# A two-block model kernel: the first half of x loaded in two pieces

## What is computed

```python
x = jax.random.normal(ks[0], (BATCH, SEQ, D_MODEL), f32)      # 1 x 256 x 1024
for layer in range(DEPTH):
    h = rms_norm(x, norm_w[layer])
    proj = h @ w_in[layer]
    ...
    x = x + merged @ w_out[layer]
```

## Time and profile before

| what | value |
|---|---|
| median of three runs | 771.51 us |
| the profiled execution's own time | 772.12 us |
| its span, first to last instruction | 770.4 us |
| PE busy | 762.7 us, 99% of the span |
| DVE busy | 556.1 us, 72% |
| ACT busy | 469.0 us, 61% |
| mean granted TensorE clock | 0.999 |
| HBM read | 147.76 MB, 193 GB/s over the span |

### The profile page before, as it was taken

One profiled execution on the slowest core, in us unless ns is written; L12 is line 12 of the kernel. 1 busy time (PEld: TensorE's weight loads), 2 busy tenths in 40 slices (PEclk: granted clock), 3 DMA queues, 4 the chain that ended last, 5 costly groups with the idle time before them and its releaser, 6 DMA issues.

```text
span 770.4 us, 12090 instructions
## 1 busy us (share of the span) xinstructions
PE 762.7 (99%) x4808; PEld 645.0 (84%) x4808; DVE 556.1 (72%) x672; ACT 469.0 (61%) x580; POOL 33.6 (4%) x62
## 2 busy tenths in 40 slices
PE   8999999999999999999999999999999999999998
PEld 8989878888998978888888998888787787878877
DVE  7898895575779797667577777458688594848865
ACT  7785596535587668644568645444575463737655
POOL 5500000000000000300000000000000000000000
PEclk9999999999999999999999999999999999999999
DMA  8666244555446435466645345654068796969921
GB/s 284 198 226 203 80 162 151 192 184 185 137 149 212 162 116 186 137 218 165 211 146 183 117 157 170 212 176 152 1 246 300 256 373 231 358 250 374 351 99 55
DMA packets 70040, 149.60 MB, mean 194 GB/s; under 512 B 8458, under 2 KB 11104, under 8 KB 69984
## 3 DMA queue, kind: packets, MB, share of 16 engines
q1 hardware_dynamic: 69568, 148.78, 56.3%
q0 software_dynamic: 384, 0.04, 0.2%
q10 hardware_dynamic: 32, 0.01, 0.0%
HBM read 147.76 MB, written 1.05 MB: 193 GB/s over the span
## 4 chain that ended last, share of the span: by engine, by line
PE 95%; DVE 1%; DMA 1%; ACT 1%; issue 0%; SPq 0%; POOL 0%; DVEq 0%; POOLq 0%; ACTq 0%
PE mm L646 19%; PE mm L648 18%; PE mm L647 18%; PE mm L662 4%; PE mm L663 4%; PE mm L664 4%; PE aux L1188 4%; PE aux L1190 4%; PE aux L1189 4%; PE aux L757 3%; PE aux L646 1%; PE aux L648 1%; PE aux L647 1%; DMA sb_raw<-in_w_up 1%; PE aux L797 1%; PE aux L1174 1%
## 5 line engine op out<-in xcount | busy, mean ns | idle before, releaser
L1831 DVE TENSOR_TENSOR sb_w_lo<-sb_raw,sb_w_hi 128x2048 fp32r<-128x2048 f32 (+2 forms) x148 | 306.7, 2081 | 85.0 <-ACT sb_w_hi L1314 41.5
L1314 ACT ACTIVATE sb_w_hi<-sb_raw 128x2048 fp32r<-128x2048 f32 (+1 forms) x83 | 155.4, 1872 | 117.6 <-PE mm L648 88.3
L646 PE MATMUL mm<-sb_w_hi,sb_hT_hi 128*128 128x512 f32 (+1 forms) x456 | 176.0, 386 | 0.0
L647 PE MATMUL mm<-sb_w_lo,sb_hT_hi 128*128 128x512 f32 (+1 forms) x456 | 172.8, 379 | 0.0
L648 PE MATMUL mm<-sb_w_hi,sb_hT_lo 128*128 128x512 f32 (+1 forms) x456 | 172.8, 379 | 0.0
L1656 ACT ACTIVATE sb_w_hi<-sb_raw 128x2048 fp32r<-128x2048 f32 x44 | 84.3, 1918 | 41.3 <-DMA sb_raw<-in_w_up 26.4
L646 PEld LDWEIGHTS mm<-sb_w_hi,sb_hT_hi 128*128 128x128 f32 x456 | 85.9, 188 | 17.3 <-issue 2.0
L648 PEld LDWEIGHTS mm<-sb_w_hi,sb_hT_lo 128*128 128x128 f32 x456 | 85.9, 188 | 16.2
L647 PEld LDWEIGHTS mm<-sb_w_lo,sb_hT_hi 128*128 128x128 f32 x456 | 86.0, 189 | 14.9
L662 PE MATMUL mm<-sb_hT_hi,sb_w_hi 128*128 128x256 f32 x272 | 78.4, 288 | 0.0
L663 PE MATMUL mm<-sb_hT_lo,sb_w_hi 128*128 128x256 f32 x272 | 77.0, 283 | 0.0
(11 more groups left out here) (429 smaller groups left out, 1136.6 us busy)
## 6 DMA issues: line engine op xcount, KB each, us to landing
sb_raw<-in_w_in SPq DMA_DIRECT2D x120, 512.0 KB, 4.6
sb_raw<-in_w_down SPq DMA_DIRECT2D x32, 512.0 KB, 5.7
sb_raw<-in_w_gate SPq DMA_DIRECT2D x31, 512.0 KB, 5.2
sb_raw<-in_w_up SPq DMA_DIRECT2D x31, 512.0 KB, 6.9
sb_raw<-in_w_out SPq DMA_DIRECT2D x16, 512.0 KB, 4.3
sb_raw<-in_w_up_attn SPq DMA_DIRECT2D x8, 512.0 KB, 4.4
sb_raw<-in_w_up_hgrn SPq DMA_DIRECT2D x8, 512.0 KB, 4.3
sb_raw<-in_w_o SPq DMA_DIRECT2D x8, 512.0 KB, 4.2
```

Of the source, the lines that this page charges most:

```text
L646: pe.matmul(dst, a_hi, rhs[0], start=start, stop=False, skip_group_check=True)
L647: pe.matmul(dst, a_hi, rhs[1], start=False, stop=False, skip_group_check=True)
L1314: act.activation(w_hi[:, slot(t), 0:width], raw[:, slot(t), 0:width], ACT.Copy).then_inc(hi_split, 1)
L1831: return dve.tensor_tensor(out_, a, b, op)
```

## The change

The first half of x comes in two transfers of 256 columns, each with a semaphore of its own. The second half is now the third transfer, with the third semaphore. PE waits for the first piece, transposes feature tiles 0 and 1, waits for the second piece, and transposes feature tiles 2 and 3. DVE waits for both pieces where it waited for the half; POOL and SP use the third semaphore for the second half.

```diff
-        in_x = [sem(f"in_x{h}") for h in range(2)]
+        in_x = [sem(f"in_x{i}") for i in range(3)]
...
-        def load_x(engine, h):
-            c = slice(h * W, (h + 1) * W)
-            engine.dma_start(x[:, :, c], A["x"].rearrange("(t p) d -> p t d", p=P)[:, :, c]).then_inc(in_x[h], 16)
+        def load_x(engine, i):
+
+            c = (slice(0, 256), slice(256, W), slice(W, D))[i]
+            engine.dma_start(x[:, :, c], A["x"].rearrange("(t p) d -> p t d", p=P)[:, :, c]).then_inc(in_x[i], 16)
...
             load_x(sp, 0)
+            load_x(sp, 1)
             for layer in range(2):
...
                         if layer == 0:
-                            load_x(sp, 1)
+                            load_x(sp, 2)
...
-            pool.wait_ge(in_x[1], 16)
+            pool.wait_ge(in_x[2], 16)
...
             pe.wait_ge(in_x[0], 16)
             begin((1, 1))
             for k in range(4):
+                if k == 2:
+                    pe.wait_ge(in_x[1], 16)
                 for tt in range(TT):
...
-            for h in range(2):
-                dve.wait_ge(in_x[h], 16)
-                dve.sem_inc(x_ready, 1)
+            dve.wait_ge(in_x[0], 16)
+            dve.wait_ge(in_x[1], 16)
+            dve.sem_inc(x_ready, 1)
+            dve.wait_ge(in_x[2], 16)
+            dve.sem_inc(x_ready, 1)
```

## The result

| | median us | runs | lowest to highest |
|---|---|---|---|
| before | 772.08 | 19 | 770.78 to 772.93 |
| with the change | 773.71 | 18 | 772.12 to 775.55 |

The medians differ by 1.63 us. The ratio that was measured is 1.0023, 95% interval 1.0016 to 1.0030, which is 1.2 to 2.3 us. (One more run of the change, at 1266.33 us with a mean granted clock of 0.557, is left out.) The prediction said 771.4, between 770.6 and 772.7; the result lies outside, on the slower side, and the prediction gave 0.05 to more than 1.54 us slower. Of the 2.3 us between 771.4 and 773.71, 0.57 is the kernel before itself: its median is 772.08 over these 19 runs, where the three runs known before gave 771.51. The profiled execution took 773.23 us, with a span of 771.5, against 772.12 and 770.4.

What follows compares the result with a forecast made beforehand. The prediction took TensorE (95% of the chain) to bound the kernel, so the edit could pay only in the ramp. Terms 0 + 0 + 0 - 0.1 = -0.1 us took the median 771.51 to 771.4, range 770.6 to 772.7.

Steps and rivals of the forecast that it cites:

- The start of PE: PE's first transposes: the first piece lands at 3.7 to 3.9, but keep-busy work holds PE until 4.68; gain 0.
- the bound of 6.0: Latest landing of the second piece of x, if a 1 KB row costs what a 2 KB row costs; 4.7 expected.
- The norm rows: Norm weights at PE's start, sharing DMA engines with x: a few hundredths to a tenth earlier, taken as -0.1 us.
- The added waits: Extra semaphore waits on PE, DVE and POOL in the ramp: each taken as 0.
- The bytes of x: First half of x in 1 KB rows at 361 GB/s for 389: 1.45 us for 1.35, so about 0.1 later.
- the one on SyncE's queue: Extra issue ahead of all weights, about 0.5 us: hidden because DMA engines set landings, which move only 0.1 (0 to 1.35).
- The margin at ACT: First weights of tile 0 land at 6.0 and ACT wants them at 6.79: margin 0.8.
- Rival 3: 1 KB rows cost more, so weight tile 2 is late beyond its 0.57 us margin: up to +0.8, 772.3; chance 0.08.
- Rival 4: TensorE's clock rises later, after an idle gap waiting for the second piece of x: +2.2, 773.6; chance 0.05.
- Rivals 1 and 2: 1: unprofiled, PE waits for x, 770.7, chance 0.10; 2: second piece waits out the first, +0.2, 771.7, chance 0.03.

## Why the prediction was wrong

**The start of PE (gain 0): right.** First transpose at 4.63 for 4.68; pieces at 3.7 and 4.4, predicted 3.7 to 3.9 and 4.7, though the second came at 5.0 and 5.4 in the repeats, inside the bound of 6.0. PE waited for neither in three profiles. The norm rows moved PE by -0.06 for the -0.1 taken, but the kernel with only the waits shows the same 3.61, so it may be chance. The added waits: 0, as said. One sentence beside the sum needs a limit: the 2.0 us of the Trainium skill, DMA: Bandwidth & Descriptors, section Anatomy of one DMA, is given there for transfers that GpSimd issues, and those of x are issued by SyncE; nothing in the sum used it.

**The bytes of x (+0.1): right for x itself, and no bound for what follows it.** While the short rows were read the rate was 357, 343 and 313 GB/s; the prediction took 361. But behind the two pieces with rows of 2 KB the weights landed at 6.2 to 7.0 (three profiles), and behind those with rows of 1 KB at 6.9 to 8.7 (five). So the short rows do cost something, in the transfer behind them.

**The step that failed** is the one on SyncE's queue: "That is hidden by the backlog", with "They move only by the 0.1 (0 to 1.35) above". The landings of before, 1.7 apart for issues 0.5 apart, were read as a backlog that sets the times alone. Then an issue 0.5 us later would be free. It was not: the weights landed 1.5, 2.1 and 2.6 us later, beyond the bound in all three. The bound was made from bytes only, and held no term for the issue itself, which the same paragraph had just priced at 0.5. One row of 2 KB, an issue with no bytes, moved them by 1.4 in its one profile, and pieces with rows of 2 KB by 0.3 to 1.1; the short rows go with about 1 us more than that. Issuing the piece behind the first weights or on ScalarE's queue, with all its short rows, moved them back to within 0.3 of before.

**The margin at ACT (0.8): right.** Weights at 5.95, wanted at 6.79, and the first product moves once they are more than about 1.0 late. A lateness of 1.5 to 2.6 less 1.0 gives +0.5 to +1.6 at the first product; measured +0.50, +1.04 and +1.55 against the first profile of before, +1.03 in the mean.

**Rival 3** (weights later, up to +0.8, 0.08) had the right kind of loss, late weights, but the wrong tile and size: not tile 2 but the first weights, and more of it. **Rival 4** (clock later, 773.6, 0.05) had the right time to 0.1 us by luck. Its wait for x was in none of the three profiles, and the clock rose at 5.2, 6.0 and 7.9, no later than before; what one of them shows is another thing, a fall at 9.4 after PE's idle gap before the first product. Rivals 1 and 2: no sign of either, the pieces landed 0.7, 1.4 and 1.8 apart, not 2.8.

**How the 1.63 adds up.** The three profiles give +1.0 at the first product and +1.25 near 200 us (the same weight load of PE, +0.42, +2.20, +1.12; the two repeats of before are at +0.05 and -0.11). At 560 us it is +1.36 (before: +0.17 and 0.00), so nearly all of this is made in the ramp. Where the rest comes from is not shown. It can lie in the clock. Over 29 runs of the change and the 105 of before that have a clock on record:

| mean granted clock | change, us (runs) | before, us (runs) | difference |
|---|---|---|---|
| 0.999 and 1.000 | 773.20 (8) | 771.99 (65) | +1.21 |
| 0.997 and 0.998 | 773.48 (14) | 772.52 (40) | +0.96 |
| 0.995 and 0.996 | 774.53 (7) | none | |

Within a class the change costs about 1.1 us, near the 1.0 of the first product. Beyond that more of its runs are in the lower classes: 72% against 38%. The lowest, a quarter of its runs, has no run of before at all, and the profile with the fallen clock (0.996) belongs to it. The table orders runs after the fact; it fits the sum but does not prove it. What a class means the profiles tell: in 8 of all 18 the granted clock falls to 0.50 for 3.4 us near 585 us, far from the edit, and these are just the 8 with a mean of 0.998 or less; the one at 0.996 has this fall and the early one. Single spans scatter there too: behind 560 us the kernel that waits for both pieces fell back by 1.2 us, while one split by token tile went from +1.5 there to +0.2 at the end, and one profile of the change waited 0.98 us for DVE at 736.78. Whether the later start makes the fall near 585 likelier I did not test.

**What stays open.** Why an issue 0.4 to 0.5 us later makes a landing 0.3 to 2.6 us later. The rows show the DMA engines busy but at 166 to 323 GB/s for one to three microseconds, in the change, in the kernel with one row ahead, and on ScalarE's queue, where it falls at 2.5 to 3.5 us (237 GB/s) and is over before the weights are due. Before has no such stretch in its three profiles (332 to 383 GB/s). Short rows are not needed for it, but it is longer and deeper with them. One thing that differs at the same time is POOL's queue: its first small rows are read from 3.7 to 4.5 us in the change and from 5.6 to 5.9 before. They are not needed for it either: with one row ahead they begin at 5.07, with ScalarE's queue at 5.9, behind the start of the slow stretch. What it is the traces do not say, nor why it is longer with the second piece of x than with a single row.

## What to carry to other kernels

A transfer that is issued earlier or split costs an issue to everything behind it in that queue, and at the start of a kernel, before the first data has landed, the landing can move by several times that issue. So before splitting a load, price the step for the next transfer in the queue, and put its lateness against the margin of the engine that waits for it; bytes alone are no bound. And nothing is gained by giving an engine one input early if it is not waiting for it, or if its next input is not earlier too. Last, a loss of 0.2% needs more than one profile of each kernel to be explained: the same kernel's first weights landed at 7.49, 8.03 and 8.54.

## What was unexpected of the hardware

- The landing of a transfer at the start is not its place in a backlog of bytes: in its profile a single 2 KB row ahead moved 512 KB of weights from 5.9 to 7.3 us.
- The DMA engines can be busy (share 0.81 to 1.05) and move only 221 to 285 GB/s, where before moved 369 to 383 in the same stretches.
- TensorE idle for 2.56 us, and its clock went to half just after the products had begun; with 1.88 and 1.44 us it did not fall there. The stretches' clock column reads 1.00 before the engine has ever been at its upper level, so the steps of equal instructions are the surer sign: 0.22 us low, 0.12 high.
